# Moving the split of w_out, spreading the zero writes and moving the start addresses of TensorE's buffers

## The reference

```python
for l in range(DEPTH):                                   # 2 layers
    h = rms_norm(x, norm_pre[l])
    proj = h @ w_in[l]                                   # its columns are shared out to three mixers
    a = mlstm_mixer(...)                                 # 4 heads x 64, forward and backward, chunks of 128
    b = gqa_mixer(...)                                   # 6 query heads, 2 key/value heads, full softmax
    c = dilated_mixer(...)                               # 6 heads, windows (128,1), (512,4), (2048,16)
    y = concatenate([a, b, c], axis=-1) @ w_out[l]       # each mixer times its own SiLU gate
    x = x + rms_norm(y, norm_post[l])
```

## The kernel before

| buffers | remainder |
|---|---|
| h_lo, w_out_hi, w_out_lo, pl_kboth0, pl_kone0, pl_qhi20, pl_qlom0, ga_qhi21 to 24 | 448 |
| h_hi, pj_w, pj_whi, pj_wlo | 288 |
| fi_mhi, fi_mlo | 256 |
| pl_ident, ga_kboth1, ga_kone1, ga_vhi, ga_vlo, ga_qlom1 to 4, ga_phi, ga_plo, ident | 128 |
| dl_q, dl_kv, ml_qk, ml_kv | 448 |
| dl_s, dl_pt, dl_v_t | 32 |
| ml_at, ml_kw, ml_w, ml_mb | 0 |

## Time and profile before

### The profile page before, as it was taken

One profiled execution on the slowest core, in us unless ns is written; L12 is line 12 of the kernel. 1 busy time (PEld: TensorE's weight loads), 2 busy tenths in 40 slices (PEclk: granted clock), 3 DMA queues, 4 the chain that ended last, 5 costly groups with the idle time before them and its releaser, 6 DMA issues. The chain is left out here.

```text
span 4000.6 us, 56871 instructions
## 1 busy us (share of the span) xinstructions
PE 3753.8 (94%) x20128; PEld 3369.0 (84%) x20128; DVE 2270.8 (57%) x4273; ACT 2035.1 (51%) x4141; POOL 1236.6 (31%) x966
## 2 busy tenths in 40 slices
PE   8999999999899997969989999999999999988698
PEld 8999999999777776857789999999987777768577
DVE  5233335512788885867652333355127888859675
ACT  5233334621787776346452333346217877763464
POOL 0000011000677766435400000110006777754354
PEclk9999999999999998879989999999999999989799
DMA  5644344332111112646444443443321111126464
GB/s 157 172 127 142 119 149 156 100 83 81 47 37 33 30 34 53 184 137 184 138 151 125 130 141 112 157 159 91 88 80 45 33 32 33 31 61 183 131 190 137
DMA packets 467163, 427.15 MB, mean 107 GB/s; under 512 B 104160, under 2 KB 425152, under 8 KB 463808
## 3 DMA queue, kind: packets, MB, share of 16 engines
q1 hardware_dynamic: 466592, 422.48, 35.9%
q10 hardware_dynamic: 288, 1.05, 0.1%
HBM read 277.65 MB, written 136.32 MB: 103 GB/s over the span
## 5 line engine op out<-in xcount | busy, mean ns | idle before, releaser
L1593 POOL TENSOR_TENSOR ga_plo<-ga_prob,ga_phi 128x512 fp32r<-128x512 f32 (+1 forms) x594 | 766.2, 1299 | 1021.2 <-ACT ga_prob L1535 1007.3
L687 PE MATMUL pj_acc<-h_hi,pj_whi 128*128 128x384 f32 x2976 | 1036.0, 348 | 8.2 <-DVE h_lo L1068 4.6
L687 PE MATMUL pj_acc<-h_lo,pj_whi 128*128 128x384 f32 x2976 | 1011.0, 340 | 0.0
L687 PE MATMUL pj_acc<-h_hi,pj_wlo 128*128 128x384 f32 x2976 | 1007.0, 338 | 0.0
L1615 DVE TENSOR_REDUCE pl_mx<-ga_ps_x 128x1 f32<-128x512 f32 (+1 forms) x760 | 511.4, 679 | 177.6 <-PE ga_ps_x L1476 164.3
L687 PEld LDWEIGHTS pj_acc<-h_hi,pj_whi 128*128 128x128 f32 x2976 | 561.4, 189 | 16.1 <-DVE h_lo L1068 5.1
L1533 ACT ACTIVATE ga_phi<-ga_ps_s 128x512 fp32r<-128x512 f32 (+1 forms) x792 | 469.9, 593 | 198.9 <-PE ga_ps_s L1493 192.7
L687 PEld LDWEIGHTS pj_acc<-h_lo,pj_whi 128*128 128x128 f32 x2976 | 561.5, 189 | 7.2
L687 PEld LDWEIGHTS pj_acc<-h_hi,pj_wlo 128*128 128x128 f32 x2976 | 561.3, 189 | 0.0
L1535 ACT ACTIVATE ga_prob<-ga_ps_s 128x512 f32<-128x512 f32 (+1 forms) x792 | 465.0, 587 | 19.3 <-DVE ga_plo L1593 17.7
L1306 POOL TENSOR_TENSOR rq_sw<-rq_sw,rq_trig 128x384 f32<-128x384 f32 x48 | 53.4, 1112 | 1255.1 <-DMA rq_sw<-pj_ring 1255.1
(11 more groups left out here) (228 smaller groups left out, 6654.0 us busy)
## 6 DMA issues: line engine op xcount, KB each, us to landing
pj_w<-in_w_in SPq DMA_DIRECT2D x62, 512.0 KB, 3.7
dl_kv<-dil_kv SPq DMA_DIRECT2D x108, 256.0 KB, 3.0
proj<-pj_ring SPq DMA_DIRECT2D x132, 192.0 KB, 2.5
fi_z<-proj SPq DMA_DIRECT2D x36, 640.0 KB
rq_trig<-in_trig SPq DMA_DIRECT2D x48, 384.0 KB, 4.0
gqk<-rq_parts SPq DMA_DIRECT2D x48, 384.0 KB, 3.1
ml_mb<-gate_M SPq DMA_DIRECT2D x72, 256.0 KB, 4.8
y<-fi_xo SPq DMA_DIRECT2D x36, 512.0 KB, 3.2
```

The source lines that it names most:

```text
L687: mm = pe.matmul(acc[s % 2][:, 0:CHUNK], wt[u][:, t, :], ht[:, t, tok], start=(t == 0 and i == 0), stop=(t == KT - 1 and i == 2))
L1593: vector.tensor_tensor(p_lo[r][:, 0:w], prob[f % 2][:, 0:w], p_hi[r][:, 0:w].bitcast(F32), ALU.subtract).then_inc(sem, 1)
```

## The change

It has four parts.

1. `SPLIT_AT` and `SECOND_AT` are 16 tiles later: 24 i + 19 in place of 24 i + 3, and 24 i + 31 in place of 24 i + 15. The loads of the halves from the third on are tied to `SPLIT_AT` and move with it; the first two are still issued as the stage begins.
2. The zero writes come group by group: the four margins and two query halves of the first group in slots 14 to 19, those of the second in 32 to 37, of the third in 50 to 55, and the four halves of `mqk` in slots 84 to 87. `load_block` waits at the first block of each group for the writes up to that group.
3. Three unused buffers (`pj_pad`, `ga_pad`, `pad`: 40, 80 and 16 elements in each partition), and another order of allocation in `lead_buffers` and `finish`.
4. Nothing else: every instruction computes what it did, on the same shapes.

```diff
 def lead_buffers(k, ctx, prefix):
...
-    return (*keys, *queries, pair(k, ctx, prefix + "mx", [P, 4, 4]), pair(k, ctx, prefix + "nmax", [P, 4, 2], F32R),
-            sbuf(k, ctx, prefix + "ident", [P, P], F32R), sbuf(k, ctx, prefix + "v0", [P, NT, HD]))
+    ident, v0 = sbuf(k, ctx, prefix + "ident", [P, P], F32R), sbuf(k, ctx, prefix + "v0", [P, NT, HD])
+    return (*keys, *queries, pair(k, ctx, prefix + "mx", [P, 4, 4]), pair(k, ctx, prefix + "nmax", [P, 4, 2], F32R), ident, v0)
+NZERO = 6
+def zeroed_at(i):
+    return NPRE + 2 + i // NZERO * 18 + i % NZERO if i < NG * NZERO else NPRE + 72 + i % NZERO
 # project
+        sbuf(k, ctx, "pj_pad", [P, 40])
         h_hi = sbuf(k, ctx, "h_hi", [P, KT, TOK], F32R)
...
-                        if L == 0:
-                            sp.wait_ge(zeros_in, len(regions) * DMA)
+                    if L == 0:
+                        sp.wait_ge(zeros_in, (g + 1) * NZERO * DMA)
...
-                for dst, src in regions[s - NPRE::NCH] if s < NPRE + NCH else []:
-                    sp.dma_start(dst, src).then_inc(zeros_in, DMA)
+                for i in range(len(regions)):
+                    if s == zeroed_at(i):
+                        sp.dma_start(*regions[i]).then_inc(zeros_in, DMA)
 # attend_gqa
         lead_buffers(k, ctx, "ga_lead_")
+        sbuf(k, ctx, "ga_pad", [P, 80])
...
-        SPLIT_AT = [24 * i + 3 for i in range(WHALVES)]
-        SECOND_AT = [24 * i + 15 for i in range(6)]
+        SPLIT_AT = [24 * i + 19 for i in range(WHALVES)]
+        SECOND_AT = [24 * i + 31 for i in range(6)]
 # finish: m_hi and m_lo are now allocated first, mgain last
+        m_hi = pair(k, ctx, "fi_mhi", [P, KT, P], F32R)
+        m_lo = pair(k, ctx, "fi_mlo", [P, KT, P], F32R)
         gpost = sbuf(k, ctx, "fi_gpost", [P, D_MODEL])
-        mgain = sbuf(k, ctx, "fi_mgain", [P, 2])
...
 # encoder
         decay = sbuf(k, ctx, "decay", [P, 2, 2, NT])
+        sbuf(k, ctx, "pad", [P, 16])
```

More of the change, by code:

```diff
@@ L158, in lead_buffers, with halves @@
     queries = [sbuf(k, ctx, prefix + n, [P, QC], F32R) for n in ("qhi20", "qlom0")]
-    return (*keys, *queries, pair(k, ctx, prefix + "mx", [P, 4, 4]), pair(k, ctx, prefix + "nmax", [P, 4, 2], F32R),
-            sbuf(k, ctx, prefix + "ident", [P, P], F32R), sbuf(k, ctx, prefix + "v0", [P, NT, HD]))
+    ident, v0 = sbuf(k, ctx, prefix + "ident", [P, P], F32R), sbuf(k, ctx, prefix + "v0", [P, NT, HD])
[3 more added lines that the diff above has]
+    return NPRE + 2 + i // NZERO * 18 + i % NZERO if i < NG * NZERO else NPRE + 72 + i % NZERO
 def zero_regions(k, zeros):
-    regions = [(k.a["dil_kv"][g, c, :, a:a + SIDE], zeros[:])
-               for g in range(NG) for a in (0, SIDE + TOK) for c in range(2)]
-    for planes in [k.a["mqk"][2 * r:2 * r + 2] for r in range(2)] + [k.a["dil_q"][g] for g in range(NG)]:
+    def halves(planes):
         for e in range(2):
             rows = slice((1 - e) * HD, (2 - e) * HD)
-            regions.append((planes[e, rows, :].rearrange("d (n t) -> d n t", t=SIDE),
-                            zeros[rows, :].unsqueeze(1).to_broadcast([HD, TOK // SIDE, SIDE])))
-    return regions
+            yield (planes[e, rows, :].rearrange("d (n t) -> d n t", t=SIDE),
+                   zeros[rows, :].unsqueeze(1).to_broadcast([HD, TOK // SIDE, SIDE]))
+    groups = [[(k.a["dil_kv"][g, c, :, a:a + SIDE], zeros[:]) for a in (0, SIDE + TOK) for c in range(2)]
+              + list(halves(k.a["dil_q"][g])) for g in range(NG)]
+    return [region for group in groups for region in group] + [
+        region for r in range(2) for region in halves(k.a["mqk"][2 * r:2 * r + 2])]
 ROTATED = [CT_GK, CT_GQ, CT_GQ + 1, CT_GQ + 2]
@@ L1911, in finish @@
         am = sbuf(k, ctx, "fi_am", [P, 2, 2])
-        m_hi = pair(k, ctx, "fi_mhi", [P, KT, P], F32R)
-        m_lo = pair(k, ctx, "fi_mlo", [P, KT, P], F32R)
         mix = sbuf(k, ctx, "fi_mix", [P, KT, P])
@@ L1917, in finish @@
         yst = sbuf(k, ctx, "fi_yst", [P, 4])
+        mgain = sbuf(k, ctx, "fi_mgain", [P, 2])
         ps_y = [psum(k, ctx, f"fi_ps_y{u}", [P, D_MODEL]) for u in range(2)]
```

## The result

The changed kernel takes 3929.48 us (median of 4 runs, 3921.9 to 3930.49), the kernel before 3998.40 (4 runs): a ratio of 0.9827, 95% interval 0.981 to 0.9844. So it is 69 us faster. The prediction was 3786 with a range of 3750 to 3980: the direction is right and the time lies in the range, but 213 us of gain were forecast, three times what came. That it lies there is luck: the range spans several cases, and the time falls into none of their own ranges (3740 to 3836, 3860 to 3925, 3966 to 3982).

A forecast was written before the change was run, and what follows sets the result against it. TensorE, busy 94% of 4000.6 us, was taken to set the pace nearly everywhere. Terms 116.6 + 58 + 12 + 21.0 + 5.4 = 213 us gave 3786 us from a 3998.5 median, with an 8-in-10 range of 3750 to 3980.

The forecast's parts named there:

- If the start is the cause, each 384-wide matmul falls to 162 ns and each 512-wide one to 215.3: All full-clock fp32r matmuls: starting operands on a multiple of 512 bytes shortens them from 175.5 and 233.5 ns.
- The excess of 13.5 and 18.2 ns: Full-clock fp32r matmuls of 384 and 512 columns: time above 162 and 215.3 ns, taken as removable by alignment.
- the fastest tile: Attention tile at 1272.00 us: 1.36 us, 227 ns per matmul, at starts off 512 like all others.
- Projection, 116.6 us forecast: Projection, 8928 matmuls of 384 columns: padding saves 13.5 ns each, discounted for early waits; bounds 108 and 120.5 us.
- the prediction's third rival: All fp32r matmuls: equal operand starts make reads meet, 4.5 ns more each, 69 us, total 4041 us; chance 0.07.
- Attention, 58 forecast: Attention, 768 tiles: 0.101 us less each, 77.6 us, three quarters counted for VectorE and ScalarE waits; bounds 40 and 77.6.
- Final stage, 12 forecast: Final stage, 1728 matmuls: 18.2 ns less each, 31 us, mostly lost to ScalarE's load waits; bounds 0 and 31.
- Later splits, 21.0 forecast: Attention's start, both layers: casting w_out 16 tiles later removes TensorE's stall and half-clock stretch; bounds 18 and 22.4 us.
- Zero writes, 5.4 forecast: First layer, 86 to 142 us: spreading zero writes brings it to the second layer's pace; bounds -4 and 6.5 us.
- Each of those groups could delay a weight load: Zero writes in slots 32, 50 and 84: at most 3.6 us each, 0 to 10.8 together, priced at 0.
- The first, that alignment reaches the fastest tile: fp32r matmuls: alignment saves only 6.6 ns per 512 columns, 5.0 per 384; 103 us, total 3896 us; chance 0.15.
- The second (starts do nothing): fp32r matmuls: alignment gains nothing, only splits and zero writes give 26.4 us; total 3972 us; chance 0.28.

The follow-up runs named there:

- the first group, still at the half clock: First of the groups of 24 matmuls that TensorE runs alone behind the changed kernel's second layer; 427 ns per matmul.
- the shifted ones: Changed kernel with all padded buffers 32 bytes further, 3942.52 us; changed kernel with only the projection's split weights 96 bytes off, 3929.37 us.
- Theory C's experiment: Changed kernel with second and third groups' query zeros moved ahead of the dilated attention: 3924.71 us; again 3931.09, beside the changed kernel's 3932.49.
- the groups: Changed kernel plus a stretch where TensorE alone runs groups of 24 matmuls at various starts; 512-column fp32r took 226.7 ns with equal starts.

## Why the prediction was wrong, step by step

- **"If the start is the cause, each 384-wide matmul falls to 162 ns and each 512-wide one to 215.3": this step failed, and with it the two largest terms.** The excess of 13.5 and 18.2 ns was read as 4.5 ns per 128 columns. It is 13.3 ns per fp32r matmul, whatever its width (512, 384, 256) and start, plus 2.2 ns at 384 columns and about 6 at 512, and only the second part depends on starts. The two references that led to 162 and 215.3, plain fp32 and the half clock, both take their columns at half the rate, where the fixed part does not show: the first group, still at the half clock, gives 427 ns too, and bf16, at the full rate but half the bytes, 215.7. (A plain fp32 matmul leaves two records, 48 for the 24 of its group; the prediction's four plain matmuls were four records of two. The argument is the same by records.) Two points at two widths cannot tell a share from a fixed part with a little on top; the fastest tile, 1.36 us, was already 6 x (213.3 + 13.3).
- **Projection, 116.6 us forecast:** 15.1 measured with the new starts alone. Its main operands already had equal starts (288 and 288) in two products of three; only the product with h_lo (448 and 288, 160 by 256) was off; the prediction's third rival named 288 and 448 alone. Over all projection matmuls the interval fell from 175.6 to 173.9 ns on average, and 8928 x 1.7 is the 15 us.
- **Attention, 58 forecast:** 9.8; the usual tile fell from 1.39 to 1.36 us, not to 1.292. **Final stage, 12 forecast:** 9.9, right in size by luck, for a different sum: 5.7 ns on 1728 matmuls is 9.8, while I had 31 and counted on the chain behind it to take 19. How much of the 9.8 reached the end is not shown: with matmuls of the same length, the two final stages of the other kernels with the new starts, the shifted ones among them, are 2.5 to 12.5 us shorter than before. ScalarE's wait for the dilated results is 34.8 us now, of 38.5 before:

```profile
ACT fi_e L2047 <- DMA fi_dl<-dil_out: 34.8, 13, 3.3
```

- **Later splits, 21.0 forecast:** 23 with the order alone (12.0 and 11.2), 24 in the changed kernel. Right, the mechanism too.
- **Zero writes, 5.4 forecast:** the stretch at 86 us gained 6.1, but 4.7 was given back in slots 37, 38 and 55. "Each of those groups could delay a weight load" named the risk and priced it at nothing; what was delayed were a block's loads and stores, not a weight load (Theory C's experiment).
- **The rivals.** The first, that alignment reaches the fastest tile, is what happened: 227 ns. Its price for the projection (5.0 ns per matmul) came from scaling the tile by columns, the same mistake; with the measured 15.1 in place of its 44.6 this rival's sum gives 3925 in place of 3896. The second (starts do nothing) is refuted by the kernel with the new starts alone, 30 us faster, and by the groups, 226.7 against 233.3 ns at starts that are all multiples of 32. For it the prediction had cited the lines of 16 bytes that "SBUF — State Buffer" in the Trainium skill gives ("Specifications (TRN2)"); for fp32r at the full clock the measurement differs from what it worked out from them, and decides. The third, operands in phase collide, was backwards: equal remainders are the fast case at 512 columns, and among the fast ones at 384.

Open: why an fp32r matmul pays some 11 ns more than a bf16 one, and by what rule 384 columns fall into one of two steady gaps.

## What to carry to other kernels

Before an excess is priced as removable, split it into a part per instruction and a part per column, with at least one reference at the same rate and data type; a reference at half the rate hides the fixed part. For fp32r matmuls, give the moving and the stationary operand starts that are equal modulo 256 bytes; a multiple of 512 is one way to get there. The gain is some 3% at 512 columns and 2% or nothing at 384, where the weights 96 bytes off cost nothing. When DMAs are spread out, look at which queue entries stand behind them in the new place.

## What the runs showed of the hardware that was not expected

- fp32r at the full clock (2.4 GHz) with equal starts takes N/2.4 + 13.3 ns per matmul of N columns (226.7, 173.3, 120.0 ns at 512, 384 and 256 columns), bf16 215.7 and 109.2 at 512 and 256.
- With starts that differ modulo 256, 512 columns take 228.8 (64), 232 to 233.3 (128) or 233.3 to 234.6 ns (all others); 384 columns 173.3 to 176.7, with two steady states at a difference of 160.
- After a switch of starts the gap settles: a group with equal remainders behind another pair of starts took up to ten matmuls of 224 to 236 ns before it ran at 226.7.
